# Hybrid attention: VectorE evicts the values of two steps ago and masks the scores two steps ahead

## What is computed

```python
def hybrid_layer(x, c, ...):              # run for l = 0, 1
    z = h @ w_in
    ...
    o_mla = mla_attention(...)            # 8 heads, keys of width 96
    o_moba = moba_attention(...)          # 8 heads of width 64, relative bias
    y = concatenate([silu(g_mla) * o_mla, silu(g_moba) * o_moba]) @ w_out
    return x + gate * y

# inside either attention, for a block of 128 queries:
    s = einsum('bqhd,bkhd->bhqk', q_blk, k) * scale   (+ bias in moba)
    s = where(kpos <= qpos, s, -inf)
    p = softmax(s)
    o = einsum('bhqk,bkhd->bqhd', p, v)
```

## Time and profile before

| | |
|---|---|
| median of 3 runs | 2018.95 us (2017.39 to 2021.28) |
| profiled execution, its own time | 2015.8 us |
| its span in the trace | 2014.0 us |
| PE busy | 1886.5 us (94%) |
| DVE busy | 1561.2 us (78%) |
| ACT busy | 1163.4 us (58%) |
| mean granted TensorE clock | 0.948 |

### The profile page before, as it was taken

One profiled execution on the slowest core, in us unless ns is written; L12 is line 12 of the kernel. 1 busy time (PEld: TensorE's weight loads), 2 busy tenths in 40 slices (PEclk: granted clock), 3 DMA queues, 4 the chain that ended last, 5 costly groups with the idle time before them and its releaser, 6 DMA issues.

```text
span 2014.0 us, 25785 instructions
## 1 busy us (share of the span) xinstructions
PE 1886.5 (94%) x9376; PEld 1580.4 (78%) x9376; DVE 1561.2 (78%) x1532; ACT 1163.4 (58%) x1218; POOL 59.8 (3%) x85
## 2 busy tenths in 40 slices
PE   7989999999877999999999999999999989888987
PEld 7888678887756788888888888888888877677766
DVE  5877768887674789898897888888888976656754
ACT  5632344435473667677676776686766755545452
POOL 2000011111100000000000000000000000000000
PEclk9999899999967999999999999999999999879968
DMA  6301269995412899999999999999999954214410
GB/s 222 126 1 43 80 239 318 332 308 176 136 42 106 298 380 331 374 347 362 371 339 371 350 361 368 341 372 347 363 345 358 378 175 152 84 43 138 153 62 22
DMA packets 161948, 489.03 MB, mean 243 GB/s; under 512 B 8178, under 2 KB 13427, under 8 KB 161744
## 3 DMA queue, kind: packets, MB, share of 16 engines
q1 hardware_dynamic: 153536, 458.21, 62.6%
q0 software_dynamic: 8336, 29.81, 4.2%
HBM read 485.36 MB, written 2.62 MB: 242 GB/s over the span
## 4 chain that ended last, share of the span: by engine, by line
PE 66%; DVE 14%; issue 10%; DMA 4%; ACT 4%; POOL 0%; DVEq 0%; ACTq 0%; POOLq 0%
PE bank L1139 19%; PE bank L1141 18%; PE bank L1140 18%; DVE weights_at L1896 4%; PE bank L1630 2%; DMA BIG<-in_e_ffn_down 2%; ACT weights_at L2824 2%; DVE BIG L2241 2%; PE bank L1348 1%; PE bank L1695 1%; PE bank L1336 1%; DMA BIG<-in_e_ffn_up 1%; DMA BIG<-in_e_w_in 1%; DMA BIG<-in_w_ada 1%; PE bank L1374 1%
## 5 line engine op out<-in xcount | busy, mean ns | idle before, releaser
L2482 DVE TENSOR_TENSOR expert_weights_low<-BIG,expert_weights_high 128x2048 fp32r<-128x2048 f32 x336 | 750.4, 2288 | 56.9 <-ACT expert_weights_high L3107 56.4
L3107 ACT ACTIVATE expert_weights_high<-BIG 128x2048 fp32r<-128x2048 f32 x336 | 625.0, 1922 | 65.1 <-DMA BIG<-in_o_moe_up 38.5
L1139 PE MATMUL bank<-expert_weights_high,expert_x_high 128*128 128x512 f32 x896 | 352.4, 393 | 2.4 <-DVE expert_x_low L2547 2.3
L1141 PE MATMUL bank<-expert_weights_low,expert_x_high 128*128 128x512 f32 x896 | 350.0, 391 | 0.0
L1140 PE MATMUL bank<-expert_weights_high,expert_x_low 128*128 128x512 f32 x896 | 349.7, 390 | 0.0
L1896 DVE TENSOR_TENSOR weights_at<-BIG,weights_at 128x2048 fp32r<-128x2048 f32 (+2 forms) x100 | 219.1, 2191 | 83.0 <-ACT weights_at L2824 80.9
L2824 ACT ACTIVATE weights_at<-BIG 128x2048 fp32r<-128x2048 f32 (+2 forms) x100 | 183.6, 1836 | 167.0 <-DMA BIG<-in_e_ffn_down 42.0
L1139 PE MATMUL bank<-weights_at,x_high 128*128 128x512 f32 (+2 forms) x608 | 244.9, 403 | 22.5 <-DVE weights_at L1896 8.3
L1140 PE MATMUL bank<-weights_at,x_low 128*128 128x512 f32 (+2 forms) x608 | 239.7, 394 | 0.0
L1141 PE MATMUL bank<-weights_at,x_high 128*128 128x512 f32 (+2 forms) x608 | 239.6, 394 | 0.0
L1139 PEld LDWEIGHTS bank<-expert_weights_high,expert_x_high 128*128 128x128 f32 x896 | 168.8, 188 | 36.8 <-DVE expert_x_low L2547 2.4
(11 more groups left out here) (400 smaller groups left out, 2350.3 us busy)
## 6 DMA issues: line engine op xcount, KB each, us to landing
BIG<-in_o_moe_gate SPq DMA_DIRECT2D x112, 1024.0 KB, 5.1
BIG<-in_o_moe_up SPq DMA_DIRECT2D x112, 1024.0 KB, 5.3
BIG<-in_o_moe_down SPq DMA_DIRECT2D x112, 1024.0 KB, 5.0
BIG<-in_w_ada POOLq DMA_DIRECT2D x48, 512.0 KB, 4.8
BIG<-in_w_in SPq DMA_DIRECT2D x20, 1024.0 KB, 5.0
BIG<-in_o_w_qkv SPq DMA_DIRECT2D x12, 1024.0 KB, 5.0
BIG<-in_e_w_in SPq DMA_DIRECT2D x10, 1024.0 KB, 5.2
BIG<-in_e_ffn_gate SPq DMA_DIRECT2D x10, 1024.0 KB, 5.4
```

Of the source, the lines that this page charges most:

```text
L1139: mm(b, high_l, high_r, start=start, stop=False, skip_group_check=not check)
L1141: last = mm(b, high_l, low_r, start=False, stop=stop, skip_group_check=not check)
L2482: tt_(E_WL[q % E_SLOTS], half(q % E_SLOTS), E_WH[q % E_SLOTS].bitcast(F32), SUB).then_inc(w_low, 1)
L3107: f(E_WH[q % E_SLOTS], half(q % E_SLOTS), ACT.Copy).then_inc(w_high, 1)
```

## The change

Only VectorE's order in the 16 steps changes. At step `i` it did `masked(i + 1)`, `sums_inverted(i)`, `values_out(i - 1)`. Now it does `values_out(i - 2)`, `sums_inverted(i)`, `masked(i + 2)`. `masked(0)` and `masked(1)` stand ahead of the loop. The low parts of steps 4 and 5 come behind `masked(6)` and `masked(7)`; the gating of the moba heads goes from step 8 to step 9, and the `x_out` of step 10 from ahead of `values_out(9)` and `masked(12)` to behind `masked(12)`. No instruction is added or removed, and PE, ACT, POOL and SP keep their order.

```diff
                 masked(0)
+                masked(1)
                 for i in range(16):
-                    if i < 15:
-                        masked(i + 1)
+                    if i >= 2:
+                        values_out(i - 2)
                     sums_inverted(i)
-                    if i == 10:
-                        x_out(("yT", l), units=(2, 3))
-                    if i:
-                        values_out(i - 1)
+                    if i < 14:
+                        masked(i + 2)
                     if i in (4, 5):
                         low()
-                    elif i == 8:
+                    elif i == 9:
                         heads_gated(512, ZGB, 5)
+                    elif i == 10:
+                        x_out(("yT", l), units=(2, 3))
+                values_out(14)
                 values_out(15)
```

## The result

The changed kernel takes 1991.53 us, the median of 4 runs (1987.39 to 2001.35); the kernel before, on the same chip, took 2018.28 us. The ratio of the runs is 0.9872, with a 95% interval of 0.9831 to 0.9913. By the medians that is 26.8 us less, where 20.7 were forecast. The profiled execution took 1988.33 us with a span of 1986.5.

A forecast was written before the change was run, and what follows sets the result against it. A chain of waits, with ready scores behind an eviction not yet needed, and PE's clock bound the attention. 7.0 (moba) + 5.5 + 8.2 (MLA, layers 0 and 1) = 20.7 us off the 2018.95 median gave 1998, range 1990 to 2011.

The forecast's parts named there:

- The reading: Attention: VectorE idles 37.7 us ahead of evictions while ready scores wait for masks; that idle should fall under 15 us.
- The moba half: Attention up to the mask of step 8: ends 3.5 us earlier a layer, 7.0 us for both.
- the walk's floor: Moba half: PE's gapless work at half clock, without the low parts' hole, lets it end at most 5.5 us earlier.
- The MLA half: Attention from mask 8 to mask 15: 17.9 us a layer, gaining 5.5 us in layer 0 and 8.2 in layer 1.
- the clock's share: MLA half: a fifth of the way from 16.0 us at full clock to the half-clock value, adding 0.2 x 9.7.
- The reason given for the rise: MLA half: PE at half clock has no gap, 6.8 us of work against a loop of about 5, so the clock rises.
- The tail: From masked(15) to the output product: 6.5 us in either order, no change, the same taken for layer 1.
- Behind the stage: After the attention PE runs straight on, so the stage's gain arrives at the end of the span.
- The rule against it: Skill's rule on matmul stages cycling through PSUM banks: by it alone the MLA half stays near half clock, 2013.9.
- The first: Rival: full clock throughout the MLA half and no hole in the moba half, 28.5 us, 1990.5; chance 0.08.
- The half-clock rival: PE at half clock replaces the eviction's wait: moba gains 7.0 us, MLA -2.3 and +0.4, 2013.9; chance 0.11.
- The slower one: Rival: evictions, one step later, hold PE up to 2.3 us a step, ending at 2035 with 16 steps; chance 0.04.

The follow-up runs named there:

- E8: The changed kernel with the two low parts moved from steps 4 and 5 to the end of the loop; 1989.57 us, ratio 0.9843.
- e4: The changed kernel with the two low parts ahead of masked(6) and masked(7) instead of behind them; 1998.65 us, ratio 0.9879.
- E5: The kernel before with two added matmuls that nobody reads in every step on PE; 2006.08 us, ratio 0.9918.
- e7: The changed kernel with the row maximum taken twice in the masks of the MLA steps; 2006.64 us, ratio 0.9931 to the kernel before.
- e6: The changed kernel with two added matmuls that nobody reads in every step on PE; 1991.34 us, ratio 0.9853 to the kernel before.

## Why the prediction was right, and where it was off

**What bound the kernel.** The reading held: the eviction's wait fell from 37.7 to 7.8 us (under 15 was forecast), 5.7 of them ahead of the last three evictions of each layer, the mask of step 3 follows its scores by 1.18 us (1.3 was forecast), and a new, shorter wait for scores took its place, 0.77 us at step 3.

**The moba half.** Forecast 3.5 us a layer, measured 3.7 and 4.1 (26.75 to 23.01, 26.73 to 22.61). The walk with the rows' durations, the low parts as the only hole included, gave masks 6 and 8 within 0.2 us. E8 and e4 agree: it is the low parts' length in that stretch that counts, not whether they stand ahead of the masks or behind them; and without them e8's 21.5 and 21.6 us lie near the walk's floor (26.7 less 5.5).

**The MLA half.** Masked(8) to masked(15) was to be 17.9 us; it is 16.7 and 16.2, so 6.6 and 9.9 us were gained where 5.5 and 8.2 were forecast. The loop came out as walked. In layer 1, at a clock of 1.00, masked(8), (9), (11), (13) and (15) start at 1935.53, 1937.18, 1941.32, 1947.59 and 1951.71. The undisturbed pairs take 4.1 us (4.0 walked), the first step 1.65 (1.2 walked), and the pair with the gating 2.1 us more than the others (2.8 walked): 16.2 in all, against the walk's bound of 16.0. PE waits 1.46 us for the gating in layer 0, as named. What was mis-sized is the clock's share, a fifth of the way to the half-clock value, where the trace has 0.93 and 1.00.

The reason given for the rise, a PE at half clock without a gap, was not borne out. In layer 0 PE was busy 17.54 of 17.80 us at half clock through the moba half and was not granted more (the row in the last section). In layer 1 it had gaps, and the full clock followed before masked(8) started at 1935.53, so ahead of the MLA half:

```profile
1927.40:1934.10 6.70, 4.89 (x23) 4.08 (x23) 5.63 (x7) 5.26 (x15) 0.00 (x0) 0.50 0.50 155
1934.20:1935.50 1.30, 1.30 (x12) 1.25 (x11) 1.23 (x3) 0.38 (x1) 0.00 (x0) 1.00 0.03 13
```

That the clock would rise and hold came true; why it does stays open, and to that extent the forecast had luck.

**The tail.** "Its tail does not change" was wrong. It fell from 6.54 us to 5.26, and from 6.53 to 5.27 in layer 1, 2.5 us in all. It is a chain of exponentials, transposes, copy and values in either order, but the clock in it was 0.69 before and is 1.00 after. E5, in the old order at 1.00, has a tail of 5.26 us too. The rows are layer 0 before and after:

```profile
1795.90:1802.40 6.50, 5.00 (x26) 4.55 (x27) 2.19 (x7) 2.96 (x8) 0.00 (x0) 0.69 0.00 0
1787.50:1792.70 5.20, 4.03 (x33) 3.47 (x32) 2.45 (x8) 3.23 (x9) 0.00 (x0) 1.00 0.00 0
```

**Behind the stage.** I had let what was gained arrive and nothing more. From the output product's first matmul to the gated heads' transposes are 6.9 us before (1802.42 to 1809.33) and 5.7 after (1792.72 to 1798.40), since the old one began at half clock; about 2.5 us for both layers. The 13.3 us that have a clock of 1.00 after the change had 0.90 before:

```profile
1802.40:1815.70 13.30, 13.30 (x58) 10.71 (x57) 5.19 (x5) 3.11 (x3) 0.00 (x0) 0.90 0.00 1
```

**The sum.** 20.7 us forecast; 0.9 more from the moba half, 2.9 from the MLA half, 2.5 from the tails and 2.5 from the output product, less the 1.9 us by which the attention starts later in this trace, is 27.6 against 27.5 in the spans. Nearly all that was missing is one thing, the clock, in three places, and in two of them, the tail and the output product, it was put at nothing. The clock share alone could not have reached the result: by the prediction's own sum a share between a twentieth and a half gives 1995 to 2004 and not 1992 to 2005, and no half clock at all in the MLA halves gives 1994.5.

**The rule against it.** The MLA halves did not go back and forth: the clock held at 1.00 through PE's gaps (busy 16.7 of 21.5 us in layer 1). The kernel before did, and so did e7, whose MLA half of layer 0 ran at 1.00, 0.50, 1.00 and 0.50 in turn. The Trainium skill (TensorE: Matmul & The Clock Gate, "A second HAM failure mode: psum-queue depth-cycling") describes such a back and forth for a stage that cycles through PSUM banks; it fits the kernel before and e7, and the trace of the changed kernel does not show it. The prediction's step from there to "near half clock" went further than the rule. That the gaps decide is not shown here: PE was idle 5.3 and 3.7 us in e7's MLA halves, 3.7 and 4.8 us in those of the changed kernel.

**The rivals.** The first (1990.5) came nearest in time: its MLA halves at full clock came nearly true, the floor of the moba half did not. What was held against it, that the clock is lost at each disturbance, the changed kernel does not show: 1.00 stayed through the 1.46 us wait for the gating. The half-clock rival fell with 0.93 and 1.00. The slower one, in which the evictions hold PE, has no wait of PE for L2726 in the trace. What stays open is the spread of the changed kernel's runs, 1987 to 2006 us, for no execution of the long kind was traced; e4's trace, of 2000.75 us with longer MLA halves at a lower clock, is a hint.

## What to carry to other kernels

In a hand-ordered queue, look for the wait that has ready work of the critical loop behind it, and swap the two; walk the engines' queues with the trace's durations to see what is late next, since that walk was right to a few tenths of a microsecond here. Then ask what clock PE will be granted, stage by stage: in this stage of small matmuls holding it was worth 13.9 us and the order 10.7 on top, and it reaches past the end of the stage. A walk does not give the clock; a test with matmuls that nobody reads holds it, so that two orders can be compared, as long as the added matmuls do not become the bound themselves.

## What the runs showed that was not expected

A PE that is busy by the profile is not thereby granted the full clock. The stretch of the changed kernel from the scores of step 3 to the end of the moba half:

```profile
1754.00:1771.80 17.80, 17.54 (x79) 15.07 (x78) 13.74 (x25) 12.32 (x30) 0.00 (x0) 0.50 0.23 63
```

PE is busy 17.54 of 17.80 us at 0.50. The same half with two idle 128x256 matmuls a step is busy 19.36 of 22.00 us at 1.00 (e6). What the added matmuls bring that the stage's own work lacks, the runs don't tell.

Work that nobody needs made the kernel before faster: 0.9918 (0.9898 to 0.9939), with PE's added matmuls in every step of the attention.
